# Two of three float32r matmuls over 256 tokens merged into one of 512 columns, their halves added outside PSUM

## The reference

```python
def swiglu(h, wi, wo):
    g, u = jnp.split(h @ wi, 2, axis=-1)
    return (jax.nn.silu(g) * u) @ wo

# second block, per layer
h = rms_norm(x, g_mix[l])
proj = h @ w_in[l]                       # heads, values, convolutions, four gates
gates = jax.nn.sigmoid(gate_in + b_gate[l])
x = x + merged @ w_merge[l]
h2 = rms_norm(x, g_ffn[l])
gt = causal_dwconv(h2 @ w_ffn_gate[l], ffn_conv_w[l])
x = x + (jax.nn.silu(gt) * (h2 @ w_ffn_up[l])) @ w_ffn_down[l]
```

## Time and profile before

| what | value |
|---|---|
| device time, median of 3 executions | 3117.19 us |
| lowest and highest | 3116.61 and 3119.4 us |
| the profiled execution: span, first to last instruction | 3113.0 us |
| its own device time | not listed apart; the median lies 4.2 us above its span |
| TensorE busy in matmuls | 2859.7 us of the span |
| VectorE, ScalarE, GpSimd busy | 2014.0, 1137.6, 578.6 us |
| mean granted TensorE clock | 0.962 of full speed |
| bytes read from HBM | 423.5 MB, 136 GB/s over the span |

### The profile page before, as it was taken

How to read it: one execution, slowest core, us unless ns; L and a number is a source line. 1 busy time by engine, 2 the same in 40 slices (tenths; PEclk the granted TensorE clock), 3 DMA queues, 4 the chain that set the end, 5 groups by cost and what they waited for, 6 DMA issues and landing times.

```text
span 3113.0 us, 42184 instructions
## 1 busy us (share of the span) xinstructions
PE 2859.7 (92%) x17476; PEld 2517.1 (81%) x17476; DVE 2014.0 (65%) x2884; ACT 1137.6 (37%) x1474; POOL 578.6 (19%) x448
## 2 busy tenths in 40 slices
PE   5999989978999989999898998899989988989899
PEld 3888867756888868888656998798989987989899
DVE  4667654576767676464676555976566768655665
ACT  3212144463222132221544334344444443444443
POOL 1100110012101121010100101991000139800000
PEclk8999999999999999999899999899989998999999
DMA  7556522103556444453202466353456563525465
GB/s 258 161 166 193 156 91 81 55 1 105 164 173 191 139 135 150 130 163 113 95 14 82 134 186 166 104 161 112 137 162 181 169 165 99 166 89 183 136 183 142
DMA packets 593166, 427.28 MB, mean 137 GB/s; under 512 B 16848, under 2 KB 571088, under 8 KB 592720
## 3 DMA queue, kind: packets, MB, share of 16 engines
q1 hardware_dynamic: 592976, 424.59, 45.7%
HBM read 423.50 MB, written 1.05 MB: 136 GB/s over the span
## 4 chain that ended last, share of the span: by engine, by line
PE 77%; DVE 12%; ACT 5%; DMA 2%; issue 2%; POOL 1%; SPq 0%; DVEq 0%; POOLq 0%; ACTq 0%
PE ps L708 22%; PE ps L710 22%; PE ps L709 22%; DVE w_lo L1432 3%; DVE cb_sum L1929 2%; ACT w_hi L1047 2%; DVE h_hi L1558 2%; PE ps L886 1%; PE pm L906 1%; DVE scaled L1522 1%; PE ps L811 1%; PE ps L810 1%; PE ps L809 1%; PE ps L894 1%; DVE scaled L1554 1%
## 5 line engine op out<-in xcount | busy, mean ns | idle before, releaser
L708 PE MATMUL ps<-h_hi,w_hi 128*128 128x256 f32 (+1 forms) x3584 | 1178.3, 329 | 115.9 <-POOL h_lo L2063 41.7
L709 PE MATMUL ps<-h_lo,w_hi 128*128 128x256 f32 (+1 forms) x3584 | 1167.0, 326 | 0.0
L710 PE MATMUL ps<-h_hi,w_lo 128*128 128x256 f32 (+1 forms) x3584 | 1165.7, 325 | 0.0
L1432 DVE TENSOR_TENSOR w_lo<-raw,w_hi 128x2048 fp32r<-128x2048 f32 (+2 forms) x376 | 818.3, 2177 | 367.1 <-ACT w_hi L1047 364.8
L708 PEld LDWEIGHTS ps<-h_hi,w_hi 128*128 128x128 f32 x3584 | 701.1, 196 | 187.3 <-issue 79.6
L1047 ACT CAST w_hi<-raw 128x2048 fp32r<-128x2048 f32 (+2 forms) x376 | 631.1, 1678 | 510.6 <-PE ps L710 321.3
L709 PEld LDWEIGHTS ps<-h_lo,w_hi 128*128 128x128 f32 x3584 | 702.0, 196 | 49.9 <-issue 0.2
L710 PEld LDWEIGHTS ps<-h_hi,w_lo 128*128 128x128 f32 x3584 | 700.8, 196 | 50.2
L2063 POOL TENSOR_TENSOR act_lo<-sil,act_hi 128x512 fp32r<-128x512 f32 (+1 forms) x132 | 150.6, 1141 | 1496.9 <-DVE act_hi L1603 938.2
L708 PE MATMUL ps<-act_hi,w_hi 128*128 128x512 f32 (+1 forms) x1056 | 355.4, 337 | 1.4 <-POOL act_lo L2063 1.4
L709 PE MATMUL ps<-act_lo,w_hi 128*128 128x512 f32 (+1 forms) x1056 | 354.8, 336 | 0.0
(11 more groups left out here) (275 smaller groups left out, 2990.2 us busy)
## 6 DMA issues: line engine op xcount, KB each, us to landing
chunk_w<-in_ada_t SPq DMA_DIRECT2D x128, 512.0 KB, 4.0
raw<-in_w_in SPq DMA_DIRECT2D x62, 1024.0 KB, 5.3
raw<-in_ffn_pre_wi SPq DMA_DIRECT2D x88, 512.0 KB, 5.2
raw<-in_ffn_post_wi SPq DMA_DIRECT2D x88, 512.0 KB, 5.2
raw<-in_ffn_pre_wo SPq DMA_DIRECT2D x32, 704.0 KB, 4.5
raw<-in_ffn_post_wo SPq DMA_DIRECT2D x32, 704.0 KB, 4.5
raw<-in_w_ffn_gate SPq DMA_DIRECT2D x44, 512.0 KB, 3.9
raw<-in_w_ffn_up SPq DMA_DIRECT2D x44, 512.0 KB, 5.2
```

Of the source, the lines that this page charges most:

```text
L708: pe.matmul(o, hi, x_hi[:, k, 0:N], start=k == 0, stop=False)
L709: pe.matmul(o, hi, x_lo[:, k, 0:N], start=False, stop=False)
L710: last = pe.matmul(o, weights(w_lo[u.low], u, k, m * P, P), x_hi[:, k, 0:N], start=False, stop=k == run.kc - 1)
L1432: nc.vector.tensor_tensor(w_lo[u.low][:, 0:n], whole[:, 0:n], w_hi[u.slot][:, 0:n].bitcast(F32), ALU.subtract).then_inc(lo_ready, 1)
```

## The change

Runs get a mark `wide`, set on those with N = 256 named above: gq, gwo, the feed-forward of post1, and in the second block aq, ak, iq, ik, gates 2 and 3, merge and both matrices of the feed-forward. Other runs keep three matmuls. The halves of `h`, `act` and the branch outputs become two planes of one tensor, so that one access takes chunk k of both. For a wide unit the product is two matmuls: hi weights by both planes (512 output columns, hi in columns 0 to 255 of the bank, lo in 256 to 511), then lo weights by the hi plane into columns 0 to 255. The two column halves are added when PSUM is read: ScalarE copies the upper one to SBUF (`keep_low`), VectorE adds the lower one (`join`), and the join frees PSUM. A wide `proj` adds the two halves to the residual one after the other, the second after a wait for the first.

In `heads` the epilogue is cut in two, so that `begin(i)` comes before `finish(i-1)`. In `ffn_in` the join stands ahead of `split_ahead`. In `conv_in` the joins and the taps stand ahead of `split_ahead`, the product behind it, and the rounding to `act_hi` goes from VectorE to ScalarE (`full_hi`), one unit late. Gates 2 and 3 free PSUM from VectorE, and the branch that uses them waits for `gate_kept`.

```diff
+            def product(o, u, k, m, x, N, kc):
+                hi, lo = weights(w_hi[u.slot], u, k, m * P, P), weights(w_lo[u.low], u, k, m * P, P)
+                if u.run.wide:
+                    pe.matmul(o, hi, x[:, :, k, 0:N], start=k == 0, stop=False)
+                    return pe.matmul(o[:, 0:N], lo, x[:, 0, k, 0:N], start=False, stop=k == kc - 1)
+                pe.matmul(o, hi, x[:, 0, k, 0:N], start=k == 0, stop=False)
+                pe.matmul(o, hi, x[:, 1, k, 0:N], start=False, stop=False)
+                return pe.matmul(o, lo, x[:, 0, k, 0:N], start=False, stop=k == kc - 1)
...
+            def keep_low(u, o):
+                act.wait_ge(unit_done, u.count)
+                nc.scalar.copy(o, ps[u.slot][:, 0:u.run.cols // P, SEQ:2 * SEQ]).then_inc(S["low_kept"], 1)
...
+            def join(s, u, o, signal):
+                dve.wait_ge(S["low_kept"], s.b["low_kept"] + u.j + 1)
+                nc.vector.tensor_tensor(o, ps[u.slot][:, 0:u.run.cols // P, 0:SEQ], o, ALU.add).then_inc(S[signal], 1)
...
                 def taps(u):
-                    split_ahead(u)
-                    dve.wait_ge(S["cin_ready"], u.j + (b["cin_ready"] + 1))
+                    dve.wait_ge(S["low_kept"], b["low_kept"] + u.j + 1)
+                    nc.vector.tensor_tensor(cin[:, r, CC_TAPS - 1:], ps[u.slot][:, 0, 0:SEQ], cin[:, r, CC_TAPS - 1:],
+                                            ALU.add).then_inc(S["cin_ready"], 1)
+                    nc.vector.tensor_tensor(joined[:, up, :], ps[u.slot][:, 1, 0:SEQ], joined[:, up, :],
+                                            ALU.add).then_inc(S[run.free], 1)
...
+                    split_ahead(u)
+                    dve.wait_ge(S["silu_ready"], b["silu_ready"] + u.j + 1)
+                    nc.vector.tensor_tensor(sil[:, r, 0:SEQ], sil[:, r, 0:SEQ], joined[:, up, :], ALU.mult).then_inc(S["act_full"], 1)
-                    nc.vector.tensor_copy(act_hi[:, bass.ds(u.j, 1), 0:N].rearrange("p c n -> p (c n)"),
...
+                def full_hi(j):
+                    act.wait_ge(S["act_full"], b["act_full"] + j + 1)
+                    nc.scalar.copy(act_hi[:, j, 0:SEQ], sil[:, j % RING, 0:SEQ]).then_inc(S["act_hi"], 1)
...
+                        for half in range(2):
+                            if half:
+                                dve.wait_ge(S["res_first"], s.b["res_first"] + u.j + 1)
+                            part = slice(half * SEQ, (half + 1) * SEQ)
+                            if s.gate is None:
+                                xc = xs[:, u.j * per:(u.j + 1) * per, 0:SEQ]
+                                last = nc.vector.tensor_tensor(xc, ps[u.slot][:, 0:per, part], xc, ALU.add)
...
                 def gated(u):
+                    if run.wide:
+                        join(s, u, joined[:, u.j % 2 * 2:u.j % 2 * 2 + 2, :], run.free)
                     split_ahead(u)
...
+                for i in range(run.n):
+                    begin(i)
+                    if not run.wide:
+                        finish(i)
+                    elif i:
+                        finish(i - 1)
+                if run.wide:
+                    finish(run.n - 1)
```

More of the change, by code:

```diff
@@ L384, in plan_layer1 @@
                  swap=True)
-        run = add(Run("gwo", 4, KC, 2 * P, cols_of(b_w_o[0], 0, 2 * P), "dve"))
-        Stage("proj", run=run, N=SEQ, gate=(1, 5), x="h", ready=("s_out", s.b["s_out"]))
+        run = add(Run("gwo", 4, KC, 2 * P, cols_of(b_w_o[0], 0, 2 * P), "dve", wide=True))
+        Stage("proj", run=run, N=SEQ, gate=(1, 5), x="h", ready=("s_out", s.b["s_out"])).takes(res_first=4)
         norm(SEQ, residual_of(run, 2), mod=(1, 2))
@@ L627, in x_of @@
     def x_of(s):
[L629 removed]
+        return dict(h=h_two, act=act_two, **branch_two)[s.x or "h"]
     def dest_of(s, ch):
@@ L705, in dense @@
                         pe.wait_ge(S[ready[0]], ready[1] + k + 1)
-                    o = ps[u.slot][:, m, 0:N]
-                    hi = weights(w_hi[u.slot], u, k, m * P, P)
-                    pe.matmul(o, hi, x_hi[:, k, 0:N], start=k == 0, stop=False)
-                    pe.matmul(o, hi, x_lo[:, k, 0:N], start=False, stop=False)
-                    last = pe.matmul(o, weights(w_lo[u.low], u, k, m * P, P), x_hi[:, k, 0:N], start=False, stop=k == run.kc - 1)
+                    last = product(ps[u.slot][:, m, 0:2 * N if run.wide else N], u, k, m, x, N, run.kc)
                 last.then_inc(unit_done, 1)
@@ L1061, in gate_out @@
                                                 bias=vec(f"b_gate{s.l}", s.i * KC + c))
-                last.then_inc(S[s.run.free], 1)
+                last.then_inc(S["gate_kept" if u.run.wide else s.run.free], 1)
             def ada(s):
@@ L1574, in add_on @@
                     dve.wait_ge(unit_done, u.count)
-                    if s.gate is None:
-                        xc = xs[:, bass.ds(u.j * per, per), 0:SEQ]
-                        nc.vector.tensor_tensor(xc, ps[u.slot][:, 0:per, 0:SEQ], xc, ALU.add).then_inc(S[run.free], 1)
+                    if run.wide:
+                        for half in range(2):
[5 more added lines that the diff above has]
+                                last = nc.vector.tensor_tensor(xc, ps[u.slot][:, 0:per, part], xc, ALU.add)
+                            else:
+                                for m in range(per):
+                                    c = u.j * per + m
+                                    last = nc.vector.scalar_tensor_tensor(xs[:, c, 0:SEQ], ps[u.slot][:, m, part], gate_of(c, 0),
+                                                                          xs[:, c, 0:SEQ], ALU.mult, ALU.add)
+                            last.then_inc(S[run.free if half else "res_first"], 1)
                         return
-                    layer, which = s.gate
                     for m in range(per):
@@ L1620, in heads @@
                     two = 2 * ((b["head_done"] + i) % 2)
+                    if run.wide:
+                        join(s, u, kept[:, two:two + nm, 0:SEQ], "head_kept")
                     dve.wait_ge(S["head_kept"], b["head_kept"] + i + 1)
```

168 lines of the change are left out of this document (106 added, 62 removed).

## The result

The changed kernel takes 3139.5 us (median of 4, 3137.2 to 3147.9) against 3117.8 us for the kernel before (four executions now): ratio 1.0077, 95% interval 1.0063 to 1.0091. It is 21.7 us slower, and above the forecast's range of 3107 to 3134 us.

What follows compares the result with a forecast made beforehand. TensorE, busy 92% of the span, was taken as the bound. Span 3113.0 less 24.2 gain, plus 23.9 costs and 3.9 for the clock, gave 3116.6; with 4.2 to the median, 3121 us, range 3107 to 3134.

Steps and rivals of the forecast that it cites:

- merged matmuls: Wide units on TensorE: each triple saves one matmul's 13.3 ns beside its columns, 24.2 us gained where it counts.
- six ends of first matrices, waits: TensorE waits longer for the last chunk: 2.4 us more at four `conv_in` ends, 1.3 at two `ffn_in` ends.
- clock behind the new waits: TensorE's granted clock falls to half after some new waits of about 2.9 us, costing 3.9 us in all.
- heads and gq: Short head runs have no next unit to hide the join: 5.6 us in the second block, 0.7 at gq.
- norms: The last residual ahead of each norm becomes two instructions, delaying the norms by 3.8 us in sum.
- third unit of post1, gate 2: Weight splits stand behind a join: 1.0 us more at post1's third unit, 0.3 at gate 2, twice.
- `conv_in` did not become bound by VectorE: Rival: VectorE's 5.42 us chain in `conv_in` overruns its 0.25 us of room, giving 3133 us; chance 0.12.
- three of these six: Four `conv_in` end waits of 2.9 us and two near 2.8 at ik; three charged 1.3 us for clock falls.
- GpSimd 0.73: At the `ffn_in` to `proj` ends, GpSimd's link in the chain before TensorE's last chunk takes 0.73 us.
- the clock falls after every new wait: Rival: eight clock falls of 1.3 us in place of three, heads at their upper bound: 3129 us; chance 0.18.
- a matmul over two planes costs as two: Rival: the merged matmul on TensorE gains nothing, or the 13.3 ns return elsewhere: 3145 us; chance 0.05.
- the sentence on the 2.5 ns: With the skill's 2.5 ns as a matmul's fixed share, merging gains only 4.5 us, giving 3141 us.

Runs made afterwards that it cites:

- e1: Changed kernel with the merged matmul kept for the first chunk only, other chunks as two 256-column matmuls: 3153.2 us, ratio 1.0112.
- e4: Changed kernel with nine useless 512-column matmuls laid into each wait of the six down projections: 3130.9 us, ratio 1.0043.
- e7: Changed kernel with the last units of the six feed-forward first matrices and the five short head runs not merged: 3112.3 us, ratio 0.9982.
- e6: Changed kernel with the last unit of each of the six merged feed-forward first matrices not merged: 3122.0 us, ratio 1.0011.
- e12: Changed kernel with the five short head runs not merged and nine useless matmuls in each of the six projection waits: 3123.8 us, ratio 1.0020.
- e11: e7 with the last unit of every merged down, merge and output projection also not merged: 3108.6 us, ratio 0.9970.
- e10: Changed kernel with first-block merged matmuls reading 512 side-by-side columns of one plane, so products are wrong: 3140.1 us, ratio 1.0062.

## Why the prediction was wrong

By its own steps, forecast and measured, in us:

| step | forecast | measured | by |
|---|---|---|---|
| merged matmuls | -24.2 | about -15 | e1 (12 to 15.5, scaled to all); 14.9 and 17.1 by counting slow and fast units in the two traces of the changed kernel |
| six ends of first matrices, waits | +12.2 | +14.0 | idle 4 x 2.37 and 2 x 2.27 over before |
| clock behind the new waits | +3.9 | +8.6 | e4, the six projections alone (7 to 11 by the ratios); the forecast counted ik in |
| heads and gq | +6.3 | +7 to 10 | e7 less e6, e12 less e4; falls behind their own waits are in it. Idle in the trace is 9.7 longer, less at most 2.3 of gain |
| norms | +3.8 | about +5 | e11 less e7, 3.7, and 1.1 of gain given up. Idle ahead of the norms in the trace: 3.8 longer over four of them, none at gwo, the output not counted |
| third unit of post1, gate 2 | +1.6 | +1.8 | idle 1.33 and twice 0.2 more |
| sum | +3.6 | +21 to 24 | 21.7 measured |

**Right** were the frame and the places. The saving of 13.3 ns a triple is real where a stage is fast: such stages run at exactly 5.55 and 3.81 us. `conv_in` did not become bound by VectorE: its units show no idle time. The waits stand where they were said to stand, 2.72 for 2.9 us, and the norms and the third unit cost about what they should.

**Wrong** were two sizes, and in small a third.
- *"A wide triple goes from 3 x 120.0 = 360.0 ns to 226.7 + 120.0 = 346.7 ns"*, for all of them. In the changed kernel's two traces 41 and 58 of 80 long units take 353.3 ns a pair. That is 7 to 9 us of gain that isn't there. The rows that I had showed 512 columns after 512 and 256 after 256; none showed one after the other, and I took the sum of the two without a bound.
- *"I charge 1.3 us for three of these six, 3.9 us; bounds none and 8 with those of post1."* Over seven traces with waits of 2.2 to 2.7 us at the six projections, the clock fell behind 30 of 42 of them; over six traces in which these waits were filled or under 1.3 us, behind none of 36. A fall cost up to 2.6 us, since the half clock lasted four microseconds and more in places. The price came from one fall, and the chance from a few other waits of before, some of which had no fall behind them; the count in these traces is the better base. Measured is 8.6 us at the six projections, against 3.9 with the waits at ik counted in. What decides between a fall and none behind the same wait stays open.
- *"GpSimd 0.73"* at `ffn_in` held for where it stood before, ahead of VectorE's split. The change put it behind the start of one: 2.04 us. The waits there are 2.23 and 2.30 us in place of 1.3, so twice 1.0 us more than forecast.
- In the heads the sum had nothing for the end of ak, where TensorE now waits 1.06 us in place of 0.28. At ik it had a little too much, 2.95 us a layer against 1.8 to 1.9.

The first three errors have one sign, and the range added none of them up: its upper end was the value of one rival by itself, not a sum of moderate misses. That is why 3139.5 lies outside.

The rival *the clock falls after every new wait* (3129 us, chance 0.18) named what happened: in the traced execution all six projections had a fall. Its price of 1.3 us was low, and it left the gain of the merged matmuls whole. With the 7 to 9 us that are missing there it would have said 3136 to 3138 us, an estimate from its own terms.

Two other figures came out nearer, 3145 us for *a matmul over two planes costs as two*, and 3141 us in the sentence on the 2.5 ns. Neither is the cause. e10 reads one plane and is as slow, and the units of e1 are 0.08 to 0.19 us longer than merged ones, where 2.5 ns a triple would make 0.04. The Trainium skill (TensorE: Matmul & The Clock Gate, Back-to-back issue gap) gives N/2.4 + 2.5 ns for a single matmul by itself, and other figures for a stream with a weight load each, which this kernel is; so the 2.5 ns should not have been set against this row. A number that comes out right is no evidence for its mechanism.

## What to carry to other kernels

A saving in a steady loop is worth it only if the way behind the loop is kept: leave the last unit of each stage in the old form, and such short stages as the head runs here (one to four units) altogether, and keep the rest. No run left the other stages of four units (merge, gwo, gates 2 and 3) unmerged as a whole, so for them this isn't shown. Price a new wait of TensorE with the fall of its clock as well, here 1 to 2.6 us behind 30 of 42 waits of 2.2 to 2.7 us, and none behind 1.2; useless matmuls laid into the wait buy it back. When a chain is re-ordered, look at what then runs beside each link, not only at what stands ahead of it.

## What the runs showed of the hardware

- Pairs of 512 and 256 columns with a weight load each run in one of two paces, 346.7 or 353.3 ns. Which it is changes between executions of one program, and within a stage (2943 to 3002 us in the changed kernel: three units of 5.55, then 5.66). It isn't quite free: in six traces, 13 of the eleven-unit stages of the second block changed from the faster to the slower pace on their way, and all 13 did so in the fifth unit. All 512 of a block ahead of all 256 gives one pace, 349 ns a pair on average. What decides between the two is open.
- The same wait of 2.70 us is followed by a fall of the clock or not, by the execution. It is part of why these kernels spread: the changed one over 3130.0 to 3147.9 us in ten executions, e11, with no such wait at its projections, over 3105.5 to 3110.8 in eight. It isn't all of it, since e7, which has none there either, spread over 3106.7 to 3125.3 in ten.
- A GpSimd subtraction of two SBUF operands beside VectorE's split, also of two SBUF operands, ended 0.58 and 0.59 us after that split in two kernels, whether it had started 0.16 or 0.60 us behind it (2.04 and 1.61 us, against 0.73 alone). Beside VectorE's adds out of PSUM it took 0.74. The Trainium skill (SBUF — State Buffer, Who interferes with whom) says that a VectorE instruction with two SBUF inputs contends with a GpSimd instruction that reads SBUF, and calls the port pair that they share an exclusive lock. The rows agree with the contention, and nearly with a lock: GpSimd's 0.73 us started anew behind the split would end 0.14 to 0.15 us later than it did.
